# The last norm of a two-block network taken on tokens instead of on channels

## Chip, cores and metric

The kernel runs on one core of a Trainium2 chip. The metric is device time of one launch in microseconds, the median of several runs.

## The reference, cut

Two transformer-like blocks follow one another on 256 tokens of width 1024; the second has two layers, each of which ends in a mixture of 16 experts. Behind the last layer stands one norm, and its result is the output:

```python
def rmsnorm(x, g):
    xf = x.astype(jnp.float32)
    y = xf * lax.rsqrt(jnp.mean(xf * xf, axis=-1, keepdims=True) + NORM_EPS)
    return (y * g.astype(jnp.float32)).astype(x.dtype)
...
        x = x + m_lat[..., 5, :] * ec_moe(h, w_router[i], w_exp_gate[i], w_exp_up[i], w_exp_down[i])
...
    return rmsnorm(x, g_final)
```

## The kernel before

The running sum of the network, xT, lies on chip with channels on the partitions: eight tiles of 128 channels by 256 tokens, in fp32. Each engine has its own program, written out by hand, and they meet at semaphores. SyncE issues the weights, TensorE multiplies, VectorE and ScalarE evict banks, scale and take functions. Nothing but the code's own order decides what follows what.

The weights of an expert come in six transfers of 2 MB (L1246) into a ring of six slots; a slot is filled again when the expert before has used it. The experts run one after another. For each, TensorE multiplies gate and up (L1100), turns the products (L1109), multiplies down (L1126), and scatters the rows back to the tokens (L1136) into four banks that gather all experts. When the last expert has been scattered, VectorE adds the gathered sum, times a gate, to xT in eight steps (L2351), each of which counts the semaphore moe_added.

The last norm, number 9, follows the same form as all norms before it. ScalarE squares each tile of xT (L1317). TensorE multiplies the squares with a square of ones (L510), which leaves the sum over channels on all partitions. ScalarE takes the root (L1324) into rs, 128x256, VectorE inverts it (L1716) and multiplies each tile of xT by the norm's weight, a column, and by rs (L1722). Then `output` turns the eight tiles to tokens on the partitions: four groups of four transposes (L467), each group into its own bank. ScalarE and VectorE evict two banks each into x_tm (L1308, L1669), and ScalarE issues one transfer of 1 MB to HBM (L1596) and waits for it:

```python
            def output(c):
                pe.wait_ge(sem("scaled"), KD * (c + 1))
                for j in range(4):
                    tb, half = j // 2, j % 2
                    b = G.open(pe, ("out", j))
```

Here KD is 8, TB (blocks of 128 tokens) is 2. G.open takes the next bank of a ring of four and waits until its last reader is done; G.take waits for the matmuls of a bank. All buffers named below are views of one large buffer, the arena. The weights of the norm, g_final_2, come with the other vectors in one load at the very start, and lie as columns in vcol.

Of the kernel before, what the change touches and what calls it, by code (L numbers as in the profile page):

```python
# [8 lines left out]
ACT = mybir.ActivationFunctionType  # L9
ALU = mybir.AluOpType  # L10
# [3 lines left out]
D = 1024  # L14
# [36 lines left out]
def shape_tables():  # L51
# [47 lines left out]
)  # L99
# [150 lines left out]
def build(nc, w, consts, out):  # L250
# [3 lines left out]
    with ctx:  # L254
# [5 lines left out]
        def sem(name):  # L260
            if name not in sems:
                sems[name] = ctx.enter_context(nc.semaphore(name))
            return sems[name]
# [24 lines left out]
        def ar(off, *shape):  # L288
            n = int(np.prod(shape))
            assert off + n <= AR, (off, shape)  # L290
            v = arena[:, off:off + n]
            if len(shape) == 2:
                v = v.rearrange("p (a b) -> p a b", a=shape[0])
            if len(shape) == 3:
                v = v.rearrange("p (a b c) -> p a b c", a=shape[0], b=shape[1])
            return v
# [96 lines left out]
        xc2 = ar(8192, TB, D)  # L393
        xc2T = ar(10240, KD, T)

        u_tm = ar(0, TB, D)
# [58 lines left out]
        def _(pe):  # L455
# [6 lines left out]
            def turn(name, b, srcs):  # L462

                for j, src in enumerate(srcs):
                    p = src.shape[0]
                    m = src.shape[1]
                    ins = pe.transpose(b[0:m, j * p:j * p + p], src, ident[0:p, 0:p])  # L467
                G.close(ins, name)
# [34 lines left out]
            def norm(c, second=False):  # L503

                norm_part(c, G.open(pe, ("ms", c), second), 0, KD)
# [499 lines left out]

            def output(c):

                pe.wait_ge(sem("scaled"), KD * (c + 1))
                for j in range(4):
                    tb, half = j // 2, j % 2  # L1010
                    b = G.open(pe, ("out", j))
                    turn(("out", j), b, [xT[:, half * 4 + m, tb * 128:tb * 128 + 128] for m in range(4)])

# [187 lines left out]
            experts(1, 8)  # L1201
            norm(9)
            output(9)

        @block.sync
        def _(sp):
# [72 lines left out]
            def item_used(key):  # L1279
                return lambda: sp.wait_ge(done, G.last_user[key])  # L1280
# [10 lines left out]
            ahead = [lambda n=n: used_up(0, n, N_EXP - 1) for n in range(len(between), SLOTS)]  # L1291
            send_experts(1, ahead + [item_used(key) for key, _ in between], 0, lambda: used_up(0, PIECES - 1, 1))

        @block.scalar
        def _(act):
# [282 lines left out]
            for tb in (1, 0):  # L1578
# [11 lines left out]
                act.activation(m_ss[:, 0:4], m_ss[:, 0:4], ACT.Sqrt, bias=eps, scale=1.0 / 128).then_inc(sem("m_hroot"), 1)  # L1590
            def output(c):
                for j in (1, 3):
                    evict(("out", j), x_tm[:, j // 2, 512:1024])
                for j in range(4):
                    G.read(act, ("out", j))
                act.dma_start(out[0].rearrange("(b p) d -> p b d", p=128), x_tm[:, 0:2, :]).then_inc(sem("out_sent"), 16)  # L1596
                act.wait_ge(sem("out_sent"), 16)

# [53 lines left out]
            experts(1, 8, lambda k: G.read(act, ("y", k)))  # L1652
            squares(9, xT, added(1))
            root(9)
            output(9)

        @block.vector
        def _(dve):
# [612 lines left out]
            def output():  # L2271
                for j in (0, 2):
                    evict(("out", j), x_tm[:, j // 2, 0:512])

# [90 lines left out]
            experts(1, 8)  # L2365
            norm(9, xT, vc("g_final_2", 0, KD), xT)
            output()
# [33 lines left out]
```

## Time and profile before

| what | value |
|---|---|
| median of 3 runs | 2019.0 us (2017.03 to 2023.29) |
| the profiled execution: time / span | 2022.01 us / 2020.2 us |
| mean granted TensorE clock | 0.899 |
| PE (matmul) busy | 1694.3 us (84%) |
| VectorE / ScalarE busy | 594.5 us (29%) / 412.2 us (20%) |
| HBM read / written | 569.83 MB / 1.05 MB |

Times of the profile count from the start of the span. The span runs from the first to the last instruction on the engines, and the execution's own time is a little longer. Busy shares are means over stages of quite different kind; the change concerns only what follows the last expert.

### The profile page before, as it was taken

To read this page: it belongs to the slowest core of one execution; us is meant where nothing else is said; L and a number is where in the kernel's file an instruction comes from. 1 tells how busy PE (TensorE), PEld (TensorE's weight loads), DVE (VectorE), ACT (ScalarE), POOL (GpSimd) and SP (SyncE) were. 2 spreads that over 40 slices of the span, in tenths; PEclk is the share of its full clock that TensorE was granted. 3 is DMA by queue.
4 is the path that set the end of the run, shared out by engine and by line. 5 is a ranking of instruction groups with operands and counts; after the bars stand their busy time and mean duration, and the time that the engine had idled before them with its cause. 6 is when DMAs were issued, how large, how long until landed. Compare 5 with 4: busy or idle time off the path is not lost.

```text
span 2020.2 us, 22500 instructions
## 1 busy us (share of the span) xinstructions
PE 1694.3 (84%) x9278; PEld 1081.7 (54%) x9278; DVE 594.5 (29%) x1438; ACT 412.2 (20%) x724; POOL 18.5 (1%) x26
## 2 busy tenths in 40 slices
PE   6999989999999999987788776677687976876775
PEld 4544347887888887554554443343345533432443
DVE  3243134215889735546331000000023100000002
ACT  4222141102131022222132111111123211111111
POOL 0000000000110000000000000000000000000000
PEclk8999987999999999888879988988897988888888
DMA  9525640044646944114669999999996899999994
GB/s 363 178 83 208 243 177 1 29 154 172 250 174 259 361 168 166 42 42 168 250 276 389 429 429 428 429 428 429 427 368 249 371 428 429 428 429 427 430 427 183
DMA packets 110598, 571.85 MB, mean 283 GB/s; under 512 B 9121, under 2 KB 15393, under 8 KB 85954
## 3 DMA queue, kind: packets, MB, share of 16 engines
q1 hardware_dynamic: 109488, 568.66, 69.9%
q10 hardware_dynamic: 1042, 2.24, 0.3%
q8 instruction: 48, 0.79, 0.2%
q14 instruction: 20, 0.16, 0.0%
HBM read 569.83 MB, written 1.05 MB: 283 GB/s over the span
## 4 chain that ended last, share of the span: by engine, by line
PE 60%; DMA 30%; DVE 4%; ACT 2%; issue 2%; SPq 1%; DVEq 0%; ACTq 0%
DMA ring<-in_w_exp_up_dram 29%; PE bank L459 19%; PE bank L1100 10%; PE bank L803 8%; PE bank L830 4%; PE bank L467 3%; PE bank L485 2%; PE bank L1176 1%; PE bank L846 1%; PE bank L1126 1%; PE bank L539 1%; PE bank L510 1%; PE bank L1136 1%; DMA ring<-in_w_ada_dram 1%; PE bank L549 1%
## 5 line engine op out<-in xcount | busy, mean ns | idle before, releaser
L1100 PE MATMUL bank<-ring,arena 128*32 128x512 f32 x1920 | 275.0, 726 | 207.9 <-DMA ring<-in_w_exp_up_dram 205.9
L1100 PEld LDWEIGHTS bank<-ring,arena 128*32 128x32 f32 x1920 | 74.9, 130 | 405.9 <-issue 403.1
L2335 DVE COPY arena<-bank 128x256 f32<-128x256 f32 x32 | 13.6, 425 | 607.6 <-PE bank L1116 607.6
L459 PE MATMUL bank<-ring,hT 128*128 128x512 f32 (+4 forms) x480 | 162.9, 497 | 6.5 <-issue 4.9
L803 PE MATMUL bank<-hT,ring 128*128 128x256 f32 x704 | 155.9, 384 | 4.2 <-ACT hT L1332 4.2
L803 PEld LDWEIGHTS bank<-hT,ring 128*128 128x128 f32 x704 | 135.0, 192 | 23.1 <-issue 4.6
L1126 PE MATMUL bank<-ring,arena 128*32 128x512 f32 x992 | 133.8, 687 | 1.7 <-DVE arena L2339 1.7
L459 PEld LDWEIGHTS bank<-ring,hT 128*128 128x128 f32 x480 | 88.1, 195 | 76.8 <-issue 66.6
L1622 ACT COPY arena<-bank 128x512 f32<-128x512 f32 x32 | 33.4, 1044 | 441.8 <-PE bank L1100 441.8
L1136 PE MATMUL bank<-arena 128*128 128x256 f32 x512 | 118.8, 385 | 1.8 <-DVE arena L2347 1.8
L1136 PEld LDWEIGHTS bank<-arena 128*128 128x128 f32 x512 | 94.6, 190 | 39.1 <-issue 27.5
L459 PE MATMUL bank<-hT,ring 128*128 128x256 f32 (+1 forms) x464 | 112.1, 402 | 0.0
L1087 PE MATMUL bank<-arena 128*128 128x32 f32 x960 | 109.7, 273 | 0.0
L1087 PEld LDWEIGHTS bank<-arena 128*128 128x128 f32 x960 | 109.6, 192 | 0.0
L467 PE MATMUL bank<-cst,arena 128*128 128x128 f32 (+2 forms) x414 | 67.7, 306 | 42.9 <-DVEq L2223 10.2
L459 PEld LDWEIGHTS bank<-hT,ring 128*128 128x128 f32 (+1 forms) x464 | 90.5, 196 | 24.3 <-issue 11.5
L459 PE MATMUL bank<-arena,ring 128*128 128x256 f32 x416 | 95.8, 385 | 3.5 <-DVE arena L1939 1.9
L467 PEld LDWEIGHTS bank<-cst,arena 128*128 128x128 f32 (+2 forms) x414 | 52.3, 154 | 83.2 <-issue 71.6
L1973 DVE SCALAR_TENSOR_TENSOR arena<-arena,vcol 128x256 f32<-128x256 f32 x176 | 91.9, 522 | 6.3
L459 PEld LDWEIGHTS bank<-arena,ring 128*128 128x128 f32 x416 | 80.1, 193 | 15.9 <-issue 3.2
L1308 ACT ACTIVATE arena<-bank 128x256 f32<-128x256 f32 (+2 forms) x74 | 33.5, 457 | 249.0 <-PE bank L459 134.3
L830 PE MATMUL bank<-arena,ring 128*128 128x256 f32 x352 | 78.4, 381 | 0.0
(314 smaller groups left out, 1698.6 us busy)
## 6 DMA issues: line engine op xcount, KB each, us to landing
ring<-in_w_exp_down_dram SPq DMA_DIRECT2D x62, 2048.0 KB, 17.0
ring<-in_w_exp_gate_dram SPq DMA_DIRECT2D x60, 2048.0 KB, 19.2
ring<-in_w_exp_up_dram SPq DMA_DIRECT2D x60, 2048.0 KB, 23.3
ring<-in_w_mod_dram SPq DMA_DIRECT2D x24, 2048.0 KB, 13.4
ring<-in_w_ada_dram SPq DMA_DIRECT2D x12, 2048.0 KB, 13.8
ring<-in_w_up_dram SPq DMA_DIRECT2D x10, 2048.0 KB, 11.1
ring<-in_w_in_dram SPq DMA_DIRECT2D x8, 2048.0 KB, 14.1
ring<-in_w_down_dram SPq DMA_DIRECT2D x5, 2048.0 KB, 9.2
```

The source lines that it names most:

```text
L459: ins = pe.matmul(b, lhs(k), rhs(k), start=(k == 0), stop=(k == n - 1))
L467: ins = pe.transpose(b[0:m, j * p:j * p + p], src, ident[0:p, 0:p])
L485: ins = pe.matmul(b[32 * q:32 * q + 32, :], cond[:, 0 if i < 12 else 1, k, :], x[:, k, :], start=(half == 0), stop=(half == 1), skip_group ...
L803: ins = pe.matmul(b[:, 0:T], x[:, k, j * 128:j * 128 + 128], hT[:, k, 0:T], start=(k == 0), stop=(k == KD - 1))
L830: ins = pe.matmul(acc[n // 2][:, (n % 2) * T:(n % 2) * T + T], x[:, k, n * 128:n * 128 + 128], ff[:, j, :], start=(j == 0 and n % 2 == 0), ...
L1087: ins = pe.matmul(bank[0][:, k * CAP:(k + 1) * CAP], h_tm[:, tb, k * 128:k * 128 + 128], hot[:, tb, :], start=(k + tb == 0), stop=(k == KD ...
L1100: ins = pe.matmul(bank[0][32 * q:32 * q + 32, :], xe[:, k * CAP:(k + 1) * CAP], xs[q // 2][:, o:o + 512], start=(k == 0), stop=(k == KD - ...
L1126: ins = pe.matmul(bank[2 + h][32 * q:32 * q + 32, :], act_t[:, 4 * j + q, :], x[:, q, h * 512:h * 512 + 512], start=(j == 0), stop=(j == 1 ...
L1136: ins = pe.matmul(acc[n // 2][:, (n % 2) * T:(n % 2) * T + T], dsb[:, n // 4, (n % 4) * 128:(n % 4) * 128 + 128], gates, start=False, stop ...
L1308: G.give(act.activation(to, src, func, **kw), name)
L1622: act.copy(gu.rearrange("p (k c) -> p c k", k=4), bank[0].rearrange("p (c k) -> p c k", k=4)).then_inc(sem("gu_copied"), 1)
L1973: ins = dve.scalar_tensor_tensor(y, win, tap(i, j), y, ALU.mult, ALU.add)
```

## The change

The order of the last norm and the last turn is exchanged. TensorE turns xT, the sum itself, in four groups of four transposes (channels 0 to 511 of both token blocks first), which wait only for the additions to their half. ScalarE squares each bank and sums the squares per row (per token) into one column each. VectorE multiplies each bank with the norm's weights, which now lie as a row on all partitions (final_row), adds the two halves' sums, and inverts the root that ScalarE takes of two columns. Both engines then scale half of each token block with that column. The token blocks leave in two transfers of 512 KB: SyncE issues the first, ScalarE the second. A one-element root ahead of the squares draws ScalarE's table in. SyncE also issues a new transfer behind the last expert weights, which puts the 4 KB row of weights on all 128 partitions.

```diff
--- before.py
+++ after.py
@@ -95,7 +95,7 @@
     (0, "b_ada"), (0, "norm1_g"), (0, "norm2_g"), (0, "q_norm_g"), (0, "kv_norm_g"), (0, "gla_norm_g"), (0, "conv_b"),
     (0, "c"), (0, "c_ctx"), (0, "s_pool_2"), (0, "g_hnorm_2"),
     (1, "b_mod_2"), (1, "c_2"), (1, "c_ctx_2"), (1, "g_norm1_2"),
-    (3, "w_conv_2"), (3, "g_norm2_2"), (3, "final_g"), (3, "g_final_2"),
+    (3, "w_conv_2"), (3, "g_norm2_2"), (3, "final_g"),
 )
 
 
@@ -393,6 +393,11 @@
         xc2 = ar(8192, TB, D)
         xc2T = ar(10240, KD, T)
 
+        gained = ar(2048, TB, 2, 512)
+        final_row = ar(4096, 2, 512)
+        unused = ar(5120, 4, 512)
+        halves_sq, row_root = small[:, 232:236], small[:, 236:238]
+
         u_tm = ar(0, TB, D)
         pT = ar(14336, KD, T)
 
@@ -1003,13 +1008,13 @@
             outputs_and_norm(6, even_out)
             G.over(("e_out", 0), ("e_out", 1))
 
-            def output(c):
-
-                pe.wait_ge(sem("scaled"), KD * (c + 1))
-                for j in range(4):
-                    tb, half = j // 2, j % 2
-                    b = G.open(pe, ("out", j))
-                    turn(("out", j), b, [xT[:, half * 4 + m, tb * 128:tb * 128 + 128] for m in range(4)])
+            def output(layer):
+
+                for half in range(2):
+                    pe.wait_ge(sem("moe_added"), KD * layer + 4 * half + 4)
+                    for tb in range(TB):
+                        b = G.open(pe, ("out", tb, half))
+                        turn(("out", tb, half), b, [xT[:, half * 4 + m, tb * 128:tb * 128 + 128] for m in range(4)])
 
             def experts(layer, c):
                 x = w3(weights(pe, ("router", layer)), KD, N_EXP)
@@ -1199,8 +1204,7 @@
             outputs_and_norm(8, pooled_out)
             G.over("w_grp")
             experts(1, 8)
-            norm(9)
-            output(9)
+            output(1)
 
         @block.sync
         def _(sp):
@@ -1290,6 +1294,11 @@
 
             ahead = [lambda n=n: used_up(0, n, N_EXP - 1) for n in range(len(between), SLOTS)]
             send_experts(1, ahead + [item_used(key) for key, _ in between], 0, lambda: used_up(0, PIECES - 1, 1))
+            sp.dma_start(final_row, w["final_row"].to_broadcast([128, D])).then_inc(sem("final_row_in"), 16)
+            sp.wait_ge(sem("out_scaled"), 1)
+            sp.wait_ge(sem("out_scaled_too"), 1)
+            sp.dma_start(out[0, 0:128, :], x_tm[:, 0, :]).then_inc(sem("out_sent"), 16)
+            sp.wait_ge(sem("out_sent"), 16)
 
         @block.scalar
         def _(act):
@@ -1588,13 +1597,22 @@
                     mod(35)
                 act.wait_ge(sem("m_hsq"), 2 - tb)
                 act.activation(m_ss[:, 0:4], m_ss[:, 0:4], ACT.Sqrt, bias=eps, scale=1.0 / 128).then_inc(sem("m_hroot"), 1)
-            def output(c):
-                for j in (1, 3):
-                    evict(("out", j), x_tm[:, j // 2, 512:1024])
-                for j in range(4):
-                    G.read(act, ("out", j))
-                act.dma_start(out[0].rearrange("(b p) d -> p b d", p=128), x_tm[:, 0:2, :]).then_inc(sem("out_sent"), 16)
-                act.wait_ge(sem("out_sent"), 16)
+            def output():
+                act.activation(small[:, 4:5], one, ACT.Sqrt)
+                for half in range(2):
+                    for tb in range(TB):
+                        act.activation(unused[:, 2 * half + tb, :], G.take(act, ("out", tb, half)), ACT.Square,
+                                       accum_out=halves_sq[:, 2 * half + tb:2 * half + tb + 1]).then_inc(sem("out_squares"), 1)
+                act.wait_ge(sem("out_summed"), 1)
+                act.activation(row_root, row_root, ACT.Sqrt, bias=eps, scale=1.0 / D).then_inc(sem("out_root"), 1)
+                act.wait_ge(sem("out_inverted"), 1)
+                for tb in range(TB):
+                    act.activation(x_tm[:, tb, 512:1024], gained[:, tb, 1, :], ACT.Copy,
+                                   scale=row_root[:, tb:tb + 1]).then_inc(sem("out_scaled_too"), 1)
+                act.wait_ge(sem("out_scaled"), 2)
+                act.wait_ge(sem("out_scaled_too"), 2)
+                act.dma_start(out[0, 128:256, :], x_tm[:, 1, :]).then_inc(sem("last_out_sent"), 16)
+                act.wait_ge(sem("last_out_sent"), 16)
 
             def added(layer):
                 return lambda k: act.wait_ge(sem("moe_added"), KD * layer + k + 1)
@@ -1650,9 +1668,7 @@
             for c in range(1, KD, 2):
                 evict(("p", c), pT[:, c, :], n=T)
             experts(1, 8, lambda k: G.read(act, ("y", k)))
-            squares(9, xT, added(1))
-            root(9)
-            output(9)
+            output()
 
         @block.vector
         def _(dve):
@@ -2269,8 +2285,22 @@
             add_output("eo", mc(1, 2))
 
             def output():
-                for j in (0, 2):
-                    evict(("out", j), x_tm[:, j // 2, 0:512])
+                dve.wait_ge(sem("final_row_in"), 16)
+                for half in range(2):
+                    for tb in range(TB):
+                        dve.wait_ge(sem("out_squares"), 2 * half + tb + 1)
+                        if half and tb:
+                            dve.tensor_tensor(row_root, halves_sq[:, 0:2], halves_sq[:, 2:4], ALU.add).then_inc(
+                                sem("out_summed"), 1)
+                        dve.tensor_tensor(gained[:, tb, half, :], G.take(dve, ("out", tb, half)), final_row[:, half, :],
+                                          ALU.mult).then_inc(sem("out_gained"), 1)
+                dve.wait_ge(sem("out_root"), 1)
+                dve.wait_ge(sem("out_gained"), 4)
+                dve.reciprocal(row_root, row_root).then_inc(sem("out_inverted"), 1)
+                dve.wait_ge(sem("out_inverted"), 1)
+                for tb in range(TB):
+                    dve.tensor_scalar(x_tm[:, tb, 0:512], gained[:, tb, 0, :], row_root[:, tb:tb + 1], None,
+                                      ALU.mult).then_inc(sem("out_scaled"), 1)
 
             def experts(layer, c):
                 set_gain(c - 1 - layer, mc(1 + layer, 4), vc("g_norm2_2", KD * layer, KD))
@@ -2363,7 +2393,6 @@
                 evict(("p", c), pT[:, c, :], T)
             add_output("y", gains(0))
             experts(1, 8)
-            norm(9, xT, vc("g_final_2", 0, KD), xT)
             output()
 
         @block.gpsimd
@@ -2389,7 +2418,8 @@
     arrays, w = {}, {}
     table, at = shape_tables()
     rows, vat, tiles = vector_rows(inputs)
-    laid_out = [("tables", table), ("pool", pool_table()), ("vectors", rows)]
+    laid_out = [("tables", table), ("pool", pool_table()), ("vectors", rows),
+                ("final_row", _np.reshape(inputs["g_final_2"], (1, D)))]
     for name, a in [(n, inputs[n]) for n in NAMES] + laid_out:
         a = _np.ascontiguousarray(a)
         arrays[f"in_{name}_dram"] = a
```

## Rows read from the trace of the kernel before

**Rows 1.** Windows: engines, granted clock, DMA share and GB/s, second expert stage
```profile
core 0: us, PE busy (x) PEld busy (x) DVE busy (x) ACT busy (x) POOL busy (x), PEclk, DMA share, GB/s
1500.00:1999.00 499.00, 383.12 (x2553) 203.56 (x2552) 56.42 (x161) 92.80 (x127) 0.00 (x0) 0.87 0.93 392
```

**Rows 2.** DMA of 1950 to 2021 us in 40 slices, GB/s
```profile
GB/s 425 434 443 425 425 434 425 406 425 443 425 415 448 425 425 434 425 397 425 443 434 332 46 0 0 0 0 0 0 9 0 0 0 0 0 0 0 171 404 16
```

**Rows 3.** Timeline, SyncE's queue: the last weights' issue
```profile
1969.04 0.81 SPq L1246 DMA_DIRECT2D ring<-in_w_exp_down_dram  x2
```

**Rows 4.** Chain that ended last, from the last scatter: start, us, what
```profile
1998.53 3.69 PE bank L1136 x16
2002.22 3.47 PE bank L510 x16
...
2005.71 0.48 ACT rs L1324
...
2006.29 1.76 DVE rs L1716
...
2008.08 3.27 DVE xT L1722 x8
...
2011.39 3.69 PE bank L467 x16
```

**Rows 5.** Timeline of the tail: start, us, engine, line, operation
```profile
1997.69 0.59 ACT L1631 COPY arena<-bank 128x512 f32<-128x512 f32 x1 [7.80 <-PE bank L1126]
...
1999.67 3.47 DVE L2351 SCALAR_TENSOR_TENSOR xT<-bank,modc,xT 128x256 f32<-128x256 f32 x8 [1.29 <-PE bank L1136]
...
2003.60 1.28 ACT L1324 ACT_TABLE_LOAD   x1
...
2012.55 0.69 DVE L1669 COPY arena<-bank 128x512 f32<-128x512 f32 x1 [1.21 <-PE bank L467]
...
2015.81 0.40 ACTq L1596 DMA_DIRECT2D out_dram<-arena  x1
```

**Rows 6.** Windows: the scatter's end and the final turn
```profile
2002.00:2006.00 4.00, 3.67 (x18) 2.88 (x16) 1.13 (x3) 3.10 (x6) 0.00 (x0) 1.00 0.00 0
...
2011.00:2015.00 4.00, 3.61 (x16) 3.28 (x16) 1.72 (x3) 0.60 (x1) 0.00 (x0) 0.50 0.00 0
```

**Rows 7.** Timeline: four turns of 128x128 and their first reader
```profile
1988.81 0.66 PE L1109 MATMUL bank<-cst,arena 128*128 128x128 f32 x4 [1.14 <-ACT arena L1622]
...
1989.50 0.38 ACT L1626 ACTIVATE arena<-bank 128x256 f32<-128x256 f32 x1 [0.75 <-PE bank L1109]
```

**Rows 8.** Groups of instructions, VectorE: busy, mean ns of one
```profile
L1834 DVE TENSOR_SCALAR arena<-arena,small 128x512 f32<-128x512 f32 x32 | 15.6, 487 | 1.1
...
L1771 DVE RECIPROCAL small<-small 128x1 f32<-128x1 f32 x6 | 1.0, 164 | 19.0 <-ACT small L1367 19.0
...
L2242 DVE TENSOR_TENSOR arena<-bank,arena 128x512 f32<-128x512 f32 x2 | 1.4, 691 | 3.2 <-PE bank L983 3.2
```

**Rows 9.** Groups of instructions, ScalarE
```profile
L1367 ACT ACTIVATE small<-small 128x1 f32<-128x1 f32 x6 | 1.8, 294 | 0.2
...
L1308 ACT ACTIVATE arena<-bank,vcol 128x512 f32<-128x512 f32 x2 | 1.3, 684 | 1.7 <-PE bank L467 1.7
```

**Rows 10.** Timeline, ScalarE: an operation with a sum, twice
```profile
114.68 0.69 ACT L1400 ACTIVATE arena<-bank,small 128x512 f32<-128x512 f32 x1
115.27 0.19 ACT L1400 ACTIVATION_READ_ACCUMULATOR arena<-bank,small 128x1 f32 x1
115.36 0.68 ACT L1400 ACTIVATE arena<-bank,small 128x512 f32<-128x512 f32 x1
```

**Rows 11.** DMA of 2010 to 2021 us in 40 slices, GB/s; the output's landing
```profile
GB/s 0 0 0 0 0 0 0 0 0 0 0 0 0 0 0 0 0 0 0 0 0 0 0 0 223 432 402 432 387 417 387 387 417 328 0 0 0 0 0 0
...
out_dram<-arena ACTq DMA_DIRECT2D x1, 1024.0 KB, 4.0
```

**Rows 12.** DMA issues: a row of 256 bytes put on all partitions
```profile
small<-in_g_qnorm_dram ACTq DMA_DIRECT2D x1, 32.0 KB, 5.9
```

## Prediction

> **What bounds the kernel now.** I read three views in this order: the windows, to see which resource is full in the long stage before the change; the DMA slices, to see where that stage stops; then the chain of waits and the timeline of the last 20 us. In the second expert stage the DMA engines are busy 93% of the time at 392 GB/s while TensorE's records fill 383 of 499 us [rows 1]: the weight stream sets the pace. It ends near 1989.2 us [rows 2]; the last weights were issued at 1969.04, by SyncE [rows 3]. From then on nothing streams, and the end is one serial chain [rows 4]: scatter of the last expert until 2002.22, the norm's 16 matmul records (3.47), root (0.48), reciprocal of 128x256 (1.76), eight scalings (3.27), 16 transposes (3.69), then an eviction and a transfer. The change touches only this chain, so what it is worth is read there; whatever it saves is saved whole, as no other work ends late. What no edit of the tail can touch is the 2000 us in front.
>
> The profiled execution took 2022.01 us with a span of 2020.2, so 1.8 us lie outside the span; the median of the three timed runs is 2019.0, 3.0 below that execution. I work out a difference of spans and take it off 2019.0.
>
> **When the sum is on tokens.** *Removed:* the norm's matmuls, the root and reciprocal over 128x256, the eight scalings, one table load (2003.60, hidden behind the matmuls already [rows 5]), and the wait of the turns for the last scaling. *Moved:* the 16 transposes now wait for the additions of L2351 alone. Those start at 1999.67 and end at 2003.14, 0.43 apart [rows 5], so the fourth ends near 2001.41, and TensorE is free of the scatter at 2002.1 to 2002.2 [rows 4]. The first group of four turns starts at 2002.1.
>
> The price of a turn depends on the clock. Before, TensorE had stood idle from 2005.7 to 2011.4, and the turns ran at a granted clock of 0.50 (the 1.2 GHz level): 3.69/16 = 0.23 each, and the first reader started 1.16 after the first turn (2011.39, 2012.55) [rows 4, 5, 6]. From 2002 to 2006 the clock was 1.00, after matmuls with no long gap [rows 6]. Four turns at that level reached their reader in 0.69 (1988.81 to 1989.50) [rows 7]; their cadence there is half of 0.23, so 0.43 to 0.46 for a group. I take this value, as the turns now follow the scatter directly. The two groups of the first half are then readable at 2002.8 and 2003.2; those of the second half start when the eighth addition has ended (2003.14, and 0.05 of hand-over), readable at 2003.9 and 2004.3.
>
> **Squares on ScalarE.** Four operations of 128x512 from a bank with a sum per row. The nearest rows are exponentials with a sum: 0.59 until the sum is read, 0.19 for that, the next starts 0.68 after the first [rows 10]. Starts: 2002.8, 3.45, 4.15, 4.8; the last sum is there at 4.8 + 0.78 = 2005.6. ScalarE is the slower partner here, not TensorE (four groups readable by 2004.3). The added one-element root that draws the table in costs 1.28 [rows 5] and about 0.3 [rows 9]; it runs behind the copy that ends at 1998.3 [rows 5], is over by 1999.9, and is covered by 2.9 us of idle ScalarE. Without that cover its load would stand between the sum and the root at full price.
>
> **VectorE.** Each of the four products of 128x512 (0.69 [rows 8]) waits for the squares of its bank. The third ends near 2005.65, about when the last sum arrives. Then the small addition (0.16, like the small reciprocal [rows 8]) to 2005.8, the fourth product to 2006.5, the reciprocal of two elements a row (0.16) to 2006.75. The root of two elements (0.29 [rows 9]) lies on ScalarE behind the fourth product. Queued behind that product are the reciprocal and both engines' scalings, so it is on the path. Hand-overs are 0.05 to 0.1 each, as between root and reciprocal now (2006.19 to 2006.29) [rows 4].
>
> **Scaling.** VectorE's halves take 0.49 each from SBUF [rows 8] and ScalarE's, a copy with a column as scale, 0.68 for the first [rows 9], about 0.6 for the next. ScalarE starts at 2006.8, ends its first at 2007.5 and its second at 2008.1; VectorE is earlier (2007.8).
>
> **Output.** Issue came 0.11 after the last eviction; data flowed from about 2016.74 to 2019.28 (0.93 after issue, 2.54 for 1024 KB), and the span ended 0.92 after the last data [rows 5, 11]. Now SyncE issues 512 KB near 2007.6 and ScalarE the other at 2008.2. Data start near 2008.55 and 2009.15. The second transfer meets the first on the same 16 engines, which one transfer alone keeps full (some 400 GB/s [rows 11]), so both together take the same 2.54 from the first start: 2011.1. With 0.92 the span ends at 2012.0, against 2020.2: **8.2 us less**. By steps: norm, root, reciprocal and scalings took 9.2 (2002.2 to 2011.4); turn and eviction 4.4 to the issue at 2015.8. In place of these 13.6 stand 5.4 until the first issue at 2007.6, so 8.2 less, and the output's own 4.4 stay.
>
> What speaks against two transfers is the Trainium skill, "DMA: Bandwidth & Descriptors", section Bandwidth: transfers should be at least 1 MiB to reach three quarters of the peak. Halves of 512 KB break this rule; no row of before shows a 512 KB store, and by the rule the time would be that of rival (a) below. The same page, under "Issuing engines are not separate DMA queues", says that several issuing queues share the 16 engines and gain no bandwidth, which would leave the 2.54 as it is; this trace has no two stores at once to show it.
>
> **The moved weights.** The norm's row on all partitions is 512 KB, queued on SyncE behind the last weights' issue at 1969.9 [rows 3]. In order behind them it needs 1.2 us at 430 GB/s and lands near 1991 to 1992, 11 us before the first product (2003.6). This cover is the idle DMA time behind 1989.2 [rows 2]. If it went between the weights instead, at most its own 1.2 us would come onto the path (the last gate and up weights are on it). SyncE's queue holds nothing after it but the two waits for the output. The gain's eight rows that leave the vector tile cost and save nothing measurable: that load stands at the very start, in one tile of unchanged size.
>
> **Bounds.** Cheaper: squares without the pause for the sum, 0.59 each (0.3); turns that start at 2001.9 (0.2); transfers limited by the second alone, 2009.15 + 1.27 (0.65). Together 1.2. Dearer: half clock in the turns, readable at 2003.3, then 0.85 apart, so the last sum at 2006.7 (1.1); products that start late behind sums (0.3); the second transfer's start-up paid again behind the first (0.9, rival (a)); the row in front of weights (1.2). Together 3.5.
>
> **Rivals.**
> (a) *The halves don't share the rate:* each pays its own start and end. First: 7.6 + 0.93 + 1.27 = 2009.8; the second's start-up after that, 0.93 + 1.27 + 0.92, ends the span at 2012.9; with half the rate for halves (2.54 each) at 2015.5. Times 2011.7 and 2014.3. For it: no store of this size in the trace. Against it: a token's line in the output is 4 KB before and after, and one transfer already splits over the 16 engines. This is what the skill's rule on 1 MiB would do here.
> (b) *TensorE's clock falls before the turns:* 2011.9. For it: it fell late in this same tail. Against it: only after idle time that is no longer there.
> (c) *Slower:* the row's transfer is slow. All 128 partitions read one line of 4 KB in HBM. A landing after 2003.6 costs one for one; from 2003.6 + 8.2 = 2011.8 the kernel is slower, by over 0.3% from 2018, so if it needs over 28 us behind the weights (1989.2). The nearest row is a 256-byte line put on 128 partitions, 5.9 us [rows 12], which would land at 1995 to 1996. Had it taken 30 us, it would land 15.6 late: 2026.4.
> (d) *The tail is shorter as forecast, but the stream of 2000 us in front comes out otherwise.* Its code is unchanged, yet the three runs of before lie between 2017.03 and 2023.29. A median may sit 2 us off: 2013 to 2014.
>
> **Numbers.** The forecast is 2019.0 - 8.2 = 2010.8 us. Chances: forecast as worked out, (a) in its cheap form and (b) included, all over 6 us faster: 0.76; (a) in its dear form or (d), 3 to 6 us faster: 0.20; (c) or anything else slower: 0.01, and within 6 us on the slow side another 0.03. Changes below 0.3% (6 us) can't be told from none with this kernel, so: faster 0.76, same 0.22, slower 0.02. Range: 1.2 below and 3.5 above from the bounds, widened by about 2 and 1.2 for the spread of runs: 2007.6 to 2015.5.
>
> **What the profile after would show.** The 16 turns right behind the scatter at clock 1.00, readable within about 2.2 us of its end; four square operations 0.6 to 0.7 apart, the last sum 3.4 us behind the scatter; no table load behind the additions; the row's transfer landed 10 us before its use; first output issue 5.4 us behind the scatter's end, second 0.6 later; about 4.4 us from the first issue to the end; distance from the scatter's end to the end of the span 9.8 instead of 18.0. Wrong would be: turns at 0.50, a table load between sum and root, VectorE waiting for the row, or a second transfer whose data start only when the first has ended.

## The result

The changed kernel takes 2010.61 us (median of 6 runs, 2007.24 to 2015.13), the one before 2020.12 in 6 runs (2017.03 to 2023.29). The ratio is 0.9952, with a 95% interval of 0.9938 to 0.9965: 9.7 us faster, between 7 and 12.5. Measured a second time it was 0.9960 (0.9946 to 0.9974). The forecast was 8.2 us less, 2010.8 us. The span of the profiled execution is 2005.3 us, 14.9 less than that of before; only 8.6 of these 14.9 lie in the part that the change touches, as the next sections show.

### The profile page after: what moved, and what is told of

It is laid out like the page before. It is cut to its first block, busy times and chain, and to the rows that moved or that the text cites. A ratio compares the mean times of both kernels' runs of the same rounds, so it can differ in the third digit from the quotient of the medians.

```text
span 2005.3 us, 22471 instructions
## 1 busy us (share of the span) xinstructions
PE 1686.3 (84%) x9262; PEld 1075.8 (54%) x9262; DVE 591.6 (30%) x1435; ACT 411.3 (21%) x725; POOL 18.5 (1%) x26
## 4 chain that ended last, share of the span: by engine, by line
PE 60%; DMA 30%; DVE 4%; ACT 2%; issue 2%; SPq 1%; DVEq 0%; ACTq 0%
DMA ring<-in_w_exp_up_dram 29%; PE bank L464 19%; PE bank L1105 10%; PE bank L808 8%; PE bank L835 4%; PE bank L472 3%; PE bank L490 2%; PE bank L1181 1%; PE bank L851 1%; PE bank L544 1%; PE bank L1131 1%; PE bank L515 1%; PE bank L1141 1%; DMA ring<-in_w_ada_dram 1%; PE bank L554 1%
## 5 line engine op out<-in xcount | busy, mean ns | idle before, releaser
L2365 DVE COPY arena<-bank 128x256 f32<-128x256 f32 x32 | 13.6, 424 | 612.1 <-PE bank L1121 612.1
L472 PE MATMUL bank<-cst,arena 128*128 128x128 f32 (+2 forms) x414 | 68.5, 309 | 43.1 <-DVEq L2239 10.2
L472 PEld LDWEIGHTS bank<-cst,arena 128*128 128x128 f32 (+2 forms) x414 | 52.8, 155 | 83.1 <-issue 71.3
```

## The profile after

The timeline of the tail, from the last scatter to the two issues of the output; columns as in [rows 5]:

```profile
1992.01 1.28 ACT L1601 ACT_TABLE_LOAD   x1
...
1992.24 3.69 PE L1141 MATMUL bank<-arena 128*128 128x256 f32 x16 [0.91 <-DVE arena L2377]
...
1995.77 2.23 PE L472 MATMUL bank<-cst,xT 128*128 128x128 f32 x16
1996.41 0.60 ACT L1604 ACTIVATE arena<-bank 128x512 f32<-128x512 f32 x1 [2.90 <-PE bank L472]
...
1997.30 1.89 DVE L2295 TENSOR_TENSOR arena<-bank,arena 128x512 f32<-128x512 f32 x3 [0.45 <-ACT arena L1604]
...
1998.66 0.21 ACT L1604 ACTIVATION_READ_ACCUMULATOR arena<-bank 128x1 f32 x1
1999.10 0.15 DVE L2293 TENSOR_TENSOR small<-small 128x2 f32<-128x2 f32 x1
1999.17 0.68 DVE L2295 TENSOR_TENSOR arena<-bank,arena 128x512 f32<-128x512 f32 x1
1999.29 0.29 ACT L1607 ACTIVATE small<-small 128x2 f32<-128x2 f32 x1 [0.42 <-DVE small L2293]
1999.95 0.17 DVE L2299 RECIPROCAL small<-small 128x2 f32<-128x2 f32 x1
2000.15 0.88 DVE L2302 TENSOR_SCALAR arena<-arena,small 128x512 f32<-128x512 f32 x2
2000.15 1.34 ACT L1610 ACTIVATE arena<-arena,small 128x512 f32<-128x512 f32 x2 [0.57 <-DVE small L2299]
2000.95 0.35 SPq L1300 DMA_DIRECT2D out_dram<-arena  x1
2001.58 0.35 ACTq L1614 DMA_DIRECT2D out_dram<-arena  x1
```

The clearest zero mark in every trace is the start of the last scatter (1998.53 before, 1992.24 here), since nothing behind it waits for the stream. From there to the end of the span it took 21.67 us before and takes 13.06 now: 8.6 less. The reader sees the new order. The turns (L472) start as the scatter leaves TensorE, 3.53 behind its start, and their first half needs only four additions. ScalarE's four squares run back to back from 1996.41 (the others start at 1996.99, 1997.60 and 1998.18), each with a read of its sum behind it; the last of those is the row at 1998.66. VectorE's first three products run beside them without a pause (1.89 in all), and the third ends at 1999.19, 0.3 after the last sum is read (1998.87). So the small addition at 1999.10 is held by both engines about equally: it comes 1.80 behind the first product, and in the run with the late row below, where the squares had long ended, 1.81 behind. The fourth product, 0.68 long, covers the root, and the reciprocal follows 0.37 after the root's end. Both engines scale from 2000.15 and ScalarE is last. The chain of [rows 4] (matmuls of the norm, root, long reciprocal, eight scalings, turn) is gone.

The window of the turn, columns as in [rows 1]:

```profile
1995.90:1998.00 2.10, 2.00 (x17) 1.52 (x15) 1.65 (x5) 1.59 (x5) 0.00 (x0) 1.00 0.00 0
```

The turns run at a granted clock of 1.00, against 0.50 in the second window of [rows 6]. The DMA of the last 11 us in 40 slices, and the issues, to set beside [rows 11]:

```profile
GB/s 0 0 0 0 0 0 0 0 0 0 0 0 0 0 0 0 0 0 0 0 0 0 0 0 149 417 372 402 432 358 447 417 372 417 30 0 0 0 0 0
...
out_dram<-arena SPq DMA_DIRECT2D x1, 512.0 KB, 2.6
out_dram<-arena ACTq DMA_DIRECT2D x1, 512.0 KB, 3.3
```

Both transfers lie in one block of some 2.6 us at about 400 GB/s, as the single one did. The new row of weights on all partitions, by its own line in SyncE's queue:

```profile
L1297 SPq DMA_DIRECT2D arena<-in_final_row_dram x1: 339/339/339, 1963.8 to 1963.8; - x1
...
DMA to landing us min/median/max: 22.2/22.2/22.2
```

It landed at 1986.0, 11.3 us before the first product at 1997.30 needed it.

## The experiments

In all of them two distances are read: from the start of the last scatter to the end of the span (called the tail), and from there to the steps between. Each tail is read from one profiled execution; where no ratio is given, the variant ran only this once.

**Each kernel again.** Nothing is edited.

> The kernel before, unchanged, measured against itself. Theory (all of the gain lies behind the last scatter; what differs ahead of it is chance from run to run): ratio to before within 0.3% of 1; from the last scatter's end to the end of the span 18.0 us again (15.5 on a bad day, no more than 0.3 us off); from the start to the last scatter's end anywhere within 4 us of 2002.2. Rival (the change also quickened the stream ahead, since the two profiles differ by 6.3 us there): this stretch is 2002.2 again within 1 us, and no profile of the kernel before comes near 1996.

> The changed kernel, unchanged, against before. Theory: ratio 0.9957 (8.6 us), the stretch behind the last scatter 9.4 us within 0.2, and the stretch ahead of it scattered over the same few us as that of the kernel before. Rival: the stretch ahead is near 1996 again, 6 us under before, and the ratio is near 0.993 (14.9 us).

The kernel before measured against itself gave 0.9995 (0.9984 to 1.0007). Its scatter in the chain of waits, start and duration:

```profile
1996.10 3.69 PE bank L1136 x16
```

The span was 2017.8, so the tail is 21.7 again, while the stretch ahead came out 2.4 us shorter (1996.10 instead of 1998.53). The same in the timeline of the changed kernel's second profile:

```profile
1996.98 3.69 PE L1141 MATMUL bank<-arena 128*128 128x256 f32 x16 [0.91 <-DVE arena L2377]
```

With a span of 2010.1 the tail is 13.1 again, and the stretch ahead is 4.7 us longer than in its first profile. The tails repeat to 0.1 us; what lies ahead wanders by several us in both kernels. Over all profiles here whose stream up to the last weights is the same, the last scatter starts between 1996.0 and 1998.5 in the kernel before and its variants, and between 1992.2 and 2001.0 in the changed one and its variants. So of the 14.9 us between the two first profiles 8.6 lie in the tail and 6.3 ahead of it. The expectation gave the end of the scatter a band of 4 us around 2002.2; the repeated kernel before lies in it (1999.8), and so does the second profile of the changed kernel (2000.7), but the first does not (1995.9). No last scatter of the kernel before or its variants ended near 1996 in a profile (the earliest at 1999.7), so the profiles alone don't rule out that the change quickens the stream.

The spans of all timed runs do better. With the tails taken as fixed (21.7 and 13.1), the last scatter of the kernel before starts anywhere from 1991.0 to 2002.1 (spans of 2012.7 to 2023.8) and that of the changed kernel from 1992.2 to 2000.2 (2005.3 to 2013.3). The medians are 1996.3 (17 runs) and 1996.5 (12) before, 1995.7 (6) and 1997.0 (6) after. The 6.3 us are within what either kernel does by itself. An effect of a microsecond or so on the stretch ahead can't be told: 8.6 us lie inside both intervals of the ratio, and these would let about 2 us pass either way.

**One transfer instead of two.**

```diff
-            sp.wait_ge(sem("out_scaled"), 1)
-            sp.wait_ge(sem("out_scaled_too"), 1)
-            sp.dma_start(out[0, 0:128, :], x_tm[:, 0, :]).then_inc(sem("out_sent"), 16)
-            sp.wait_ge(sem("out_sent"), 16)
...
-                act.dma_start(out[0, 128:256, :], x_tm[:, 1, :]).then_inc(sem("last_out_sent"), 16)
+                act.dma_start(out[0].rearrange("(b p) d -> p b d", p=128), x_tm[:, 0:2, :]).then_inc(sem("last_out_sent"), 16)
```

> The changed kernel with one output transfer of 1 MB, issued by ScalarE when both engines have scaled everything. Theory (two transfers share the 16 engines, and the second costs nothing that shows): the only issue comes 5.6 us behind the scatter's end instead of 5.0, then 0.93 + 2.54 + 0.92: the stretch behind the scatter is 10.0 us, 0.6 more than with two. Rival (each half pays its own start and end, or halves run at a lower rate): 9.4 us or less.

In its timeline:

```profile
1992.41 3.69 PE L1141 MATMUL bank<-arena 128*128 128x256 f32 x16 [0.91 <-DVE arena L2373]
...
2001.75 0.40 ACTq L1610 DMA_DIRECT2D out_dram<-arena  x1
```

The issue stands 9.34 behind the scatter's start, where the second issue stood with two; the span is 2006.2 and the tail 13.8. The first of two transfers is worth 0.7 us, about the 0.63 by which its issue is earlier, so the two share the engines without loss.

**Without the one-element root.**

```diff
-                act.activation(small[:, 4:5], one, ACT.Sqrt)
```

> The changed kernel without the one-element root ahead of the squares. Theory: ScalarE loads the table right behind the last square (1.28 us from 2.95 us behind the scatter's end), which ends 0.85 us after the sum is ready; the stretch behind the scatter is 10.2 us instead of 9.4. Rival 1 (the load goes ahead of the squares by itself, or is hidden behind VectorE's last product): 9.4. Rival 2 (a change of table costs a pause as long as the load besides): 11.5.

The timeline from the table load; the scatter started at 1998.36:

```profile
2005.00 1.28 ACT L1606 ACT_TABLE_LOAD   x1
2005.22 0.15 DVE L2292 TENSOR_TENSOR small<-small 128x2 f32<-128x2 f32 x1
2005.29 0.68 DVE L2294 TENSOR_TENSOR arena<-bank,arena 128x512 f32<-128x512 f32 x1
2006.30 0.30 ACT L1606 ACTIVATE small<-small 128x2 f32<-128x2 f32 x1
2006.62 0.17 DVE L2298 RECIPROCAL small<-small 128x2 f32<-128x2 f32 x1 [0.65 <-ACT small L1606]
```

The load stands where expected, behind the last sum and ahead of the wait, and no pause as long as itself follows. The load's first 0.4 us lie under the addition that the root waits for, and the root starts 0.9 us later (7.94 behind the scatter's start instead of 7.05). But the span is 2012.0, the tail 13.6, only 0.6 longer: of the 0.9 us, VectorE's fourth product hides another 0.3. The expectation (0.8 longer) had forgotten the 0.37 between root and reciprocal, of which all but the hand-over is slack.

**Two transfers on the old order.** SyncE waits for the first two banks of the turn; the rest is as before.

```diff
+            G.read(sp, ("out", 0))
+            G.read(sp, ("out", 1))
+            sp.dma_start(out[0, 0:128, :], x_tm[:, 0, :]).then_inc(sem("out_sent"), 16)
+            sp.wait_ge(sem("out_sent"), 16)
...
-                act.dma_start(out[0].rearrange("(b p) d -> p b d", p=128), x_tm[:, 0:2, :]).then_inc(sem("out_sent"), 16)
-                act.wait_ge(sem("out_sent"), 16)
+                act.dma_start(out[0, 128:256, :], x_tm[:, 1, :]).then_inc(sem("last_out_sent"), 16)
+                act.wait_ge(sem("last_out_sent"), 16)
```

> The kernel before with nothing changed but the output in two transfers of 512 KB (SyncE the first 128 tokens as soon as their two banks are evicted, ScalarE the rest). From the start of the last scatter to the end of the span it was 21.7 us. Theory: the first transfer is issued 1.7 us earlier and is over before the second one's data start, so only half the data lie behind the last issue: 20.4 us, 1.3 less, which is the part of the change's 8.6 us that two transfers alone would give on the old tail. Rival (a transfer of half the size pays back what it saves in start and end): 21.5 or more.

Timeline, and the DMA of the last 11 us:

```profile
1996.00 3.69 PE L1136 MATMUL bank<-arena 128*128 128x256 f32 x16 [0.90 <-DVE arena L2351]
...
2011.54 0.35 SPq L1295 DMA_DIRECT2D out_dram<-arena  x1
...
2013.28 0.35 ACTq L1600 DMA_DIRECT2D out_dram<-arena  x1
```

```profile
GB/s 0 0 0 0 0 0 0 0 0 0 0 0 0 0 0 0 0 0 0 0 0 0 0 0 0 119 402 402 417 432 134 0 387 432 387 417 283 0 0 0
...
out_dram<-arena SPq DMA_DIRECT2D x1, 512.0 KB, 2.6
out_dram<-arena ACTq DMA_DIRECT2D x1, 512.0 KB, 2.6
```

The span was 2016.3, the tail 20.3: 1.4 less. Here the two don't meet. The first is through before the second starts, and each moves its 512 KB at 387 to 432 GB/s and lands 2.6 us after issue, where 1024 KB took 4.0 [rows 11]. So about 1.3 us of a store, an estimate from these two times, are its start and end, and they are hidden for the first. The Trainium skill, "DMA: Bandwidth & Descriptors", section Anatomy of one DMA, puts this fixed part at about 2.0 us for the other path (GpSimd's). These stores, from SyncE and ScalarE, show less.

**The clock alone, on the old order.**

```diff
             norm(9)
+            for _ in range(50):
+                pe.transpose(bank[7][:, 0:128], ident, ident)
             output(9)
```

> The kernel before with 50 transposes without use on TensorE between the norm's matmuls and the last turn, into a bank that nothing reads any more. Theory (the turns of before took 0.23 each because TensorE had idled and its granted clock was 0.50): the clock stays at 1.00, the 16 turns take 1.7 to 1.9 us instead of 3.7, and the stretch from the last scatter's start to the end is 20.0 us, 1.7 less; the useless turns (some 5.4 us) end before the last scaling. Rival (fp32 transposes take 0.23 at either level, or the clock falls all the same): 21.7.

Timeline of the scatter and the turn, then the window of the turn:

```profile
1997.96 3.69 PE L1136 MATMUL bank<-arena 128*128 128x256 f32 x16 [0.91 <-DVE arena L2349]
...
2004.94 5.62 PE L1204 MATMUL bank<-cst 128*128 128x128 f32 x50
...
2010.82 1.73 PEld L467 LDWEIGHTS bank<-cst,xT 128*128 128x128 f32 x16 [0.50 <-DVE xT L1724]
```

```profile
2010.80:2012.80 2.00, 1.97 (x16) 1.73 (x16) 1.10 (x2) 0.60 (x1) 0.00 (x0) 1.00 0.00 0
```

The useless transposes end at 2010.56, and the turn starts 12.86 behind the scatter's start, just as before. The 16 turns take 1.97 us instead of 3.7, at a granted clock of 1.00; the span was 2017.9, the tail 19.9. So 1.7 us of the old tail were a turn at the 1.2 GHz level behind 5.7 us of idle TensorE, and the change gets them without asking, because its turn follows matmuls at once.

**Both edits on the old order.** The two diffs above together.

> The kernel before with both single edits: the 50 transposes without use that keep TensorE's clock up, and the output in two transfers. Theory (what is left of the change's gain when the old order has both is what taking the norm on tokens is worth by itself): the first transfer is issued 0.9 us before the second, they overlap, and from the last scatter's start to the end it is 19.1 us; so 2.6 us of the change's 8.6 come from clock and transfers, and 6.0 from the order. Rival (the two edits don't add up, or the order is worth less): below 18.5, or 20 and more.

```profile
1996.26 3.69 PE L1136 MATMUL bank<-arena 128*128 128x256 f32 x16 [0.91 <-DVE arena L2353]
...
2010.93 0.35 SPq L1297 DMA_DIRECT2D out_dram<-arena  x1
...
2011.84 0.35 ACTq L1602 DMA_DIRECT2D out_dram<-arena  x1
```

The span was 2015.3, the tail 19.0. The two issues are 0.9 apart, and the second transfer saves 0.9 on this quicker tail. This is as near as the old order came, and the changed kernel is 6.0 us below it. That is what the norm on tokens is worth without the clock and the second transfer.

**Eight rows behind the weights.**

```diff
+            for i in range(7):
+                sp.dma_start(ar(7168 + 1024 * i, D), w["final_row"].to_broadcast([128, D])).then_inc(sem("more_rows_in"), 16)
             sp.dma_start(final_row, w["final_row"].to_broadcast([128, D])).then_inc(sem("final_row_in"), 16)
...
+            sp.wait_ge(sem("more_rows_in"), 7 * 16)
```

> The changed kernel with the 512 KB row transfer eight times behind the last weights (seven into unused places, the needed one last). Theory (it runs in order behind the weights, in idle DMA time): the needed one lands some 8.5 us later than now, 2 us behind the scatter's start and still 3 before the first product; last scatter's start to end 13.1 us, ratio to before 0.996 as without it. Rival 1 (later transfers go between the weights already queued): the last expert's weights land late, ratio 1.000 or more. Rival 2 (reading one line for all partitions is slower than 400 GB/s): the first product waits for the row, and the stretch behind the scatter is over 14 us.

The needed row's issue, the scatter and the first product, then the time from that issue to landing:

```profile
1984.28 4.25 SPq L1299 DMA_DIRECT2D arena<-in_final_row_dram  x1
...
2001.01 3.69 PE L1141 MATMUL bank<-arena 128*128 128x256 f32 x16 [0.91 <-DVE arena L2380]
...
2006.07 1.89 DVE L2298 TENSOR_TENSOR arena<-bank,arena 128x512 f32<-128x512 f32 x3 [0.45 <-ACT arena L1607]
```

```profile
DMA to landing us min/median/max: 20.7/20.7/20.7
```

The DMA of 1960 to 2014 us in 40 slices:

```profile
GB/s 425 413 437 437 425 425 425 425 437 413 413 443 413 449 413 425 437 425 437 425 413 437 391 410 391 407 407 410 358 297 276 206 76 0 0 0 0 228 404 146
```

The tail is 13.1 and the ratio 0.9957 (0.9940 to 0.9974): nothing is lost. But the row landed at 2005.0, 4.0 us behind the scatter's start and not 2, with only 1.1 us of cover left. Counted from the scatter's start, it landed 10.2 us later than in the changed kernel, 1.46 for each of the seven rows more. That is 360 GB/s on average, not 430. The slices show how it comes about: some 400 GB/s for the first rows, then less and less over the last 7 us. What slows them stays open.

**Eight rows inside the stream.** The same transfers, the needed one last, stand before SyncE's loop over experts 3 to 15 of the second layer:

```diff
+                if layer:
+                    for i in range(8):
+                        to, arrived = (final_row, "final_row_in") if i == 7 else (ar(7168 + 1024 * i, D), "more_rows_in")
+                        sp.dma_start(to, w["final_row"].to_broadcast([128, D])).then_inc(sem(arrived), 16)
                 with sp.Fori(3, N_EXP) as e:
...
-            sp.dma_start(final_row, w["final_row"].to_broadcast([128, D])).then_inc(sem("final_row_in"), 16)
...
+            sp.wait_ge(sem("more_rows_in"), 7 * 16)
```

> The changed kernel with the same eight row transfers issued in the middle of the weight stream (before the fourth expert of the second layer) instead of behind it. Theory (the stream sets the pace there, so 4.2 MB at 428 GB/s cost what they take, 9.8 us): ratio to before 1.001 (0.996 + 0.0048), the stretch behind the last scatter's start unchanged at 13.1; one row there would cost 1.2 us. Rival (the stage has slack between transfers, and absorbs them): ratio 0.996.

```profile
2007.38 3.69 PE L1141 MATMUL bank<-arena 128*128 128x256 f32 x16 [0.91 <-DVE arena L2381]
```

The span was 2020.5, so the tail is 13.1 here too. The ratio was 1.0022 (1.0011 to 1.0034), 0.0062 above the changed kernel's second measurement, 12.5 us or 1.6 a row (the two intervals leave 1.1 to 2.0). So the stream does not absorb the rows. What a row costs fits the 1.46 of the transfers behind the weights; the 1.2 expected lies at the edge of the interval. If a single row costs an eighth of eight, which was not run, it would have taken about a fifth of the gain there; behind the last weights it is free.

**The row late.** Seven rows, a wait for them, six more, then the needed one.

```diff
+            for i in range(7):
+                sp.dma_start(ar(7168 + 1024 * i, D), w["final_row"].to_broadcast([128, D])).then_inc(sem("more_rows_in"), 16)
+            sp.wait_ge(sem("more_rows_in"), 7 * 16)
+            for i in range(6):
+                sp.dma_start(ar(7168 + 1024 * i, D), w["final_row"].to_broadcast([128, D])).then_inc(sem("more_rows_in"), 16)
             sp.dma_start(final_row, w["final_row"].to_broadcast([128, D])).then_inc(sem("final_row_in"), 16)
...
+            sp.wait_ge(sem("more_rows_in"), 13 * 16)
```

> The changed kernel with thirteen 512 KB row transfers ahead of the needed one, the last six and the needed one sent only when the first seven have landed. Theory (the row is hidden only while it lands before the first product, 5.1 us behind the last scatter's start; behind that it costs one for one): it lands some 14 us behind the scatter's start (7 further transfers at 1.3 to 1.5 us, and about 2 for the restart), 9 late, and the stretch from the scatter's start to the end is 13.1 + 9 = 22 us, which is slower than the kernel before. Rival (the transfers behind the weights are quicker, or the first product is not what waits): less than 16.

```profile
1995.74 3.69 PE L1141 MATMUL bank<-arena 128*128 128x256 f32 x16 [0.91 <-DVE arena L2383]
...
2011.66 1.89 DVE L2301 TENSOR_TENSOR arena<-bank,arena 128x512 f32<-128x512 f32 x3 [11.32 <-DMA arena<-in_final_row_dram]
2013.47 0.15 DVE L2299 TENSOR_TENSOR small<-small 128x2 f32<-128x2 f32 x1
```

VectorE's first product waited 11.32 us for the row. It started 15.92 behind the scatter's start instead of 5.06, 10.9 later, and the tail grew by the same (span 2019.7, tail 24.0 against 13.1). Lateness costs one for one, as expected; the 22 us expected were 2 too few, because the row came some 2 us later than worked out. Now the tail is longer than before the change. The mechanism of the slower rival is real; it only starts from a lateness that one row is far from: it landed 11.3 us before its use in the changed kernel.

**One product fewer.** The last bank is scaled by row and column in one operation.

```diff
                             dve.tensor_tensor(row_root, halves_sq[:, 0:2], halves_sq[:, 2:4], ALU.add).then_inc(
                                 sem("out_summed"), 1)
+                            continue
...
-                dve.wait_ge(sem("out_gained"), 4)
+                dve.wait_ge(sem("out_gained"), 3)
...
-                for tb in range(TB):
-                    dve.tensor_scalar(x_tm[:, tb, 0:512], gained[:, tb, 0, :], row_root[:, tb:tb + 1], None,
-                                      ALU.mult).then_inc(sem("out_scaled"), 1)
+                dve.tensor_scalar(x_tm[:, 0, 0:512], gained[:, 0, 0, :], row_root[:, 0:1], None,
+                                  ALU.mult).then_inc(sem("out_scaled"), 1)
+                dve.scalar_tensor_tensor(x_tm[:, 1, 512:1024], G.take(dve, ("out", 1, 1)), row_root[:, 1:2],
+                                         final_row[:, 1, :], ALU.mult, ALU.mult).then_inc(sem("out_scaled"), 1)
```

(ScalarE scales the second half of the first block and the first half of the second.)

> The changed kernel without its fourth product: VectorE leaves the bank of the second block's second half as it is, takes the reciprocal as soon as the root is there, and then scales that bank with row and column in one operation (0.75 us); ScalarE scales one half of each token block. Theory (what stands between the last sum and the first issue is VectorE's fourth product, then 1.3 us of scalings): the reciprocal starts 0.3 us earlier, both issues come 0.3 earlier, and the stretch from the last scatter's start to the end is 12.8 us instead of 13.1; ratio to before 0.996, not to be told from the changed kernel. Rival (ScalarE's path sets the end alone): 13.1.

```profile
2001.95 0.29 ACT L1607 ACTIVATE small<-small 128x2 f32<-128x2 f32 x1 [0.42 <-DVE small L2293]
2002.28 0.17 DVE L2300 RECIPROCAL small<-small 128x2 f32<-128x2 f32 x1 [0.36 <-ACT small L1607]
2002.48 1.33 ACT L1610 ACTIVATE arena<-arena,small 128x512 f32<-128x512 f32 x2 [0.23 <-DVE small L2300]
2002.48 0.49 DVE L2302 TENSOR_SCALAR arena<-arena,small 128x512 f32<-128x512 f32 x1
2002.88 0.75 DVE L2304 SCALAR_TENSOR_TENSOR arena<-bank,small,arena 128x512 f32<-128x512 f32 x1
2003.28 0.35 SPq L1300 DMA_DIRECT2D out_dram<-arena  x1
```

The reciprocal follows the root by 0.04 instead of 0.37, the first issue comes 8.37 behind the scatter's start instead of 8.71, and the tail is 12.7 (scatter from 1994.91, span 2007.6), 0.4 less than the changed kernel's. The ratio to before, 0.9963 (0.9950 to 0.9976), can't tell it from the changed kernel; only the tail in the profile can. By the tail it is the best version here.

## Why the prediction was right

- *The stage and the sum.* The tail was the right place, and its saving was had whole: 8.2 worked out, 8.6 in the trace. The 8.6 can now be told apart: 1.7 for the clock, 0.9 for the second transfer, 6.0 for the order; the old order with clock and transfers both mended keeps 19.0 of its 21.7.
- *The time itself.* That the median, 2010.61, lies 0.2 from the forecast is partly luck: the kernel before came out 1.1 us slower in six runs than in the three that the forecast started from (2020.12, 2019.0), and the medians differ by 9.5 and not by 8.2. The two nearly cancel.
- *Turn.* Right: clock 1.00, the first reader 4.17 behind the scatter's start, 4.27 forecast; the fourth addition, not the eighth, lets it start.
- *Squares.* The one term that was mis-sized by more than 0.1. Priced by exponentials with a column as bias, 0.68 apart [rows 10]; squares without one came 0.58 to 0.61 apart, the cheap bound. The last sum was there 6.6 behind the scatter's start, 7.1 forecast, and what follows came 0.3 to 0.4 earlier. Of the difference between 8.2 and 8.6 some 0.3 are the squares and 0.1 the turn. Squares cheaper still would gain little: the three products take as long, and they hold the addition too.
- *Product, root, reciprocal, scaling.* Right in sum. From the last sum to the first issue 2.0 were forecast and 2.1 passed; between the issues 0.6 and 0.63. That the root hides behind the fourth product is confirmed twice: taking the product away brings the reciprocal forward, delaying the root costs less than the delay.
- *Table load.* Covered, as forecast. "Full price" without its cover was too much: 0.6 of 1.28.
- *Output.* Shared rate, confirmed: start, 2.6 us of data, 0.9 to the end. Rival (a) fell. What the Trainium skill says in "DMA: Bandwidth & Descriptors" under "Issuing engines are not separate DMA queues" held: the two stores together ran at the one's rate. The Trainium skill's rule of 1 MiB a transfer (same page, section Bandwidth) is not borne out for these stores: each half moved at 387 to 432 GB/s, the one of 1 MB at 387 to 432 too [rows 11], and an earlier half won 0.7 us in the new order and 1.4 in the old.
- *The moved row.* Right in effect, probably a little cheap in size: some 1.5 to 1.6 us a row when eight stand in a row, and not 1.2, of which nothing shows with 11 us of cover. Rival (c) needs a landing 8.6 us later than the first product, and a run that made it 10.9 late showed a tail longer than before the change.
- *Rivals (b) and (d).* The clock did not fall. The wandering stream is real and was well sized. It is enough to explain the step from the tail's 8.6 to the medians' 9.5, which lies well inside the interval.

## What to carry to other kernels

When every engine waits in turn at the end, count the tail from a mark behind which nothing external waits; that distance repeats to 0.1 us where the total wanders by several. Put the layout change first when the next step can then work with one number per partition instead of a full tile, and ask of every small load whether it stands inside the stream that sets the pace or behind it: the same 512 KB cost some 1.6 us in one place (an eighth of what eight cost) and nothing in the other. Work that is hidden has a measurable slack, and moving it costs only what exceeds that slack.

## What the runs showed of the hardware

- 16 fp32 transposes of 128x128 take 3.68 us at a granted clock of 0.50 and 1.97 at 1.00; 50 transposes in a row without use kept the clock at 1.00 over 5.6 us in which TensorE otherwise stood idle and came back at 0.50.
- One 4 KB line read for all 128 partitions, 512 KB in all, costs some 1.46 us when eight such transfers stand behind the weights, 360 GB/s on average. The rate is about 400 GB/s at first and falls over the last 7 us; the weights run at some 425.
- ScalarE loads a table for an operation before it waits for that operation's semaphore: the load at 2005.00 started behind the last sum, while the add that the root waits for was still to come (2005.22). The root followed the load's end by 0.02.
- A square of 128x512 with a sum per row, from a bank, comes 0.58 to 0.61 us behind the one before it; the sum is there 0.69 after the start of the operation.
- A store of 512 KB from SyncE or ScalarE lands 2.6 us after its issue, one of 1024 KB 4.0; two that overlap share one rate, and the second lands after 3.3.
- SyncE's issue of a transfer takes some 0.34 us as a rule, and 4.25 us when seven rows were queued ahead of it and the last weights were still coming in. A queue behind long transfers is no cheap place for a step that others wait on.
